# A two-part transformer kernel: order of units in two attentions, one load moved forward, the last norm per token

## The reference

```python
# first attention: 4 differential heads (qa, ka, va) and 8 grouped heads (qb, kb, vb)
oa = _rmsnorm(oa, subln) * (1.0 - lam_init)          # norm per head, over 128 features
qb = _axial_rope(_rmsnorm(qb, qk_norm[0]), ang_r, ang_c)
mix = concatenate([oa, ob]); h = h + mix @ w_out
# block attention (the third): 8 heads of 128
k = rotary(k, ...); q = rotary(q, ...) ; s = where(k_pos <= q_pos, q k, -inf); o = softmax(s) v
# the end
y = x32 * rsqrt(mean(x32 * x32, axis=-1) + NORM_EPS) * g
```

## Time and profile before

| | us |
|---|---|
| runs | 1433.71, 1434.3, 1440.1 (median 1434.3) |
| profiled execution | 1434.04, its span 1432.2 |
| PE busy | 1361.8 |
| DVE busy | 804.8 |
| ACT busy | 570.3 |
| PE's granted clock, mean | 0.994 |

### The profile page before, as it was taken

How to read it: one execution, slowest core, us unless ns; L and a number is a source line. 1 busy time by engine, 2 the same in 40 slices (tenths; PEclk the granted TensorE clock), 3 DMA queues, 4 the chain that set the end, 5 groups by cost and what they waited for, 6 DMA issues and landing times.

```text
span 1432.2 us, 25229 instructions
## 1 busy us (share of the span) xinstructions
PE 1361.8 (95%) x9936; PEld 1062.6 (74%) x9936; DVE 804.8 (56%) x1440; ACT 570.3 (40%) x1006; POOL 174.3 (12%) x168
## 2 busy tenths in 40 slices
PE   7999899999999999999999999997999999998897
PEld 6776899999767999998989996443437678454343
DVE  6968877676776756667764866211117566311112
ACT  4566544444575544446334633111106354111111
POOL 2000264332100532314000010000000001000000
PEclk9999999999999999999999999999999999999999
DMA  9141274444314444453543679999997249999995
GB/s 391 63 177 60 109 282 177 177 174 177 119 60 158 177 177 184 184 206 132 190 164 118 234 301 366 399 426 426 413 417 327 107 174 412 371 419 426 423 412 220
DMA packets 42024, 355.42 MB, mean 248 GB/s; under 512 B 4918, under 2 KB 6326, under 8 KB 21440
## 3 DMA queue, kind: packets, MB, share of 16 engines
q1 hardware_dynamic: 40560, 349.34, 61.1%
q0 software_dynamic: 928, 4.30, 0.8%
q10 hardware_dynamic: 432, 0.32, 0.1%
HBM read 352.86 MB, written 1.09 MB: 247 GB/s over the span
## 4 chain that ended last, share of the span: by engine, by line
PE 75%; DMA 12%; DVE 7%; ACT 3%; issue 1%; POOL 1%; SPq 1%; DVEq 0%; ACTq 0%; POOLq 0%
PE psum L1945 14%; PE psum L1377 13%; PE psum L1379 13%; PE psum L1378 13%; DMA ring<-w_expert_dram 7%; PE psum L1924 3%; DMA constants_sb<-constants_dram 2%; PE psum L1442 2%; DMA arena<-w_expert_dram 1%; DVE weight_low L2676 1%; PE psum L1410 1%; PE psum L1779 1%; PE psum L1778 1%; PE psum L1780 1%; DMA ring<-w_dense_dram 1%
## 5 line engine op out<-in xcount | busy, mean ns | idle before, releaser
L1377 PE MATMUL psum<-x_high,weight_low 128*128 128x256 f32 (+1 forms) x1096 | 317.9, 290 | 8.3 <-DVE x_low L2816 2.4
L2676 DVE TENSOR_TENSOR weight_low<-ring,weight_high 128x1024 fp32r<-128x1024 f32 x196 | 251.1, 1292 | 114.2 <-ACT weight_high L2200 113.6
L1378 PE MATMUL psum<-x_low,weight_high 128*128 128x256 f32 (+1 forms) x1096 | 311.3, 284 | 0.0
L1379 PE MATMUL psum<-x_high,weight_high 128*128 128x256 f32 (+1 forms) x1096 | 310.6, 283 | 0.0
L2200 ACT ACTIVATE weight_high<-ring 128x1024 fp32r<-128x1024 f32 x196 | 204.8, 1055 | 147.2 <-PE psum L1379 109.7
L1377 PEld LDWEIGHTS psum<-x_high,weight_low 128*128 128x128 f32 x1096 | 205.8, 188 | 20.5 <-issue 8.2
L1378 PEld LDWEIGHTS psum<-x_low,weight_high 128*128 128x128 f32 x1096 | 206.2, 188 | 0.8 <-issue 0.5
L1379 PEld LDWEIGHTS psum<-x_high,weight_high 128*128 128x128 f32 x1096 | 206.7, 189 | 0.0
L1945 PE MATMUL psum<-ring,xn 128*32 128x512 f32 (+2 forms) x800 | 141.2, 594 | 5.7 <-DMA ring<-w_expert_dram 5.6
L1377 PE MATMUL psum<-hidden_high,weight_low 128*128 128x272 f32 (+1 forms) x512 | 145.9, 285 | 0.2 <-DVE hidden_low L2878 0.2
L1379 PE MATMUL psum<-hidden_high,weight_high 128*128 128x272 f32 (+1 forms) x512 | 146.0, 285 | 0.0
(11 more groups left out here) (411 smaller groups left out, 2485.3 us busy)
## 6 DMA issues: line engine op xcount, KB each, us to landing
ring<-w_dense_dram SPq DMA_DIRECT2D x68, 2048.0 KB, 7.7
ring<-w_expert_dram SPq DMA_DIRECT2D x30, 2048.0 KB, 23.0
ring<-w_expert_dram SPq DMA_DIRECT2D x34, 1024.0 KB, 12.3
ring<-w_expert_dram SPq DMA_DIRECT2D x64, 512.0 KB, 12.1
ahead_a<-w_expert_dram SPq DMA_DIRECT2D x6, 2048.0 KB, 9.8
arena<-w_expert_dram SPq DMA_DIRECT2D x6, 2048.0 KB, 14.3
arena<-w_expert_dram SPq DMA_DIRECT2D x22, 512.0 KB, 19.7
constants_sb<-w_expert_dram SPq DMA_DIRECT2D x5, 2048.0 KB, 16.8
```

Of the source, the lines that this page charges most:

```text
L1377: pe.matmul(o, wl[:, c % 4, cols], high, start=start, stop=False)
L1378: pe.matmul(o, wh[:, c % 4, cols], low, start=False, stop=False)
L1379: return pe.matmul(o, wh[:, c % 4, cols], high, start=False, stop=stop)
L2676: v.tensor_tensor(split_view(wl, (name, j), c), quarter_view((name, j), q), split_view(wh, (name, j), c).bitcast(F32), ALU.subtract).then_ ...
```

## The change

Four groups of edits. In the first attention the last value block moves from unit 14 to 15, its transpose from 16 to 22, the last rotation from 5 to 7, half product 6 from 24 to 23. In the block attention the transposes at s = 5 and 7 use bank 7, and SP issues the constants before `kv` 2 instead of after `kv` 3. The root's activation table is loaded in each expert stage's last step instead of at the end. The last norm sums the squares into one column for each half of the tokens, with tokens on the partitions, takes root and reciprocal of 128x2 numbers, puts them on a diagonal (`ident` times factor), and spreads them over the partitions by a product with ones into bank 2, which DVE reads in its four products. Odd chunks are stored from ACT's queue, even ones from SP's.

```diff
-    BLOCK0 = {4 * j + x: (name, j) for j in range(4) for x, name in enumerate(("qa", "ka", "va"))}
-    TURN_V0 = {4: 0, 8: 1, 12: 2, 16: 3}
-    ROT0 = {1: 1, 3: 2, 5: 3}
-    HALF0 = {n + (16 if n < 6 else 18): n for n in range(8)}
+    BLOCK0 = {4 * j + x + (4 * j + x == 14): (name, j) for j in range(4) for x, name in enumerate(("qa", "ka", "va"))}
+    TURN_V0 = {4: 0, 8: 1, 12: 2, 22: 3}
+    ROT0 = {1: 1, 3: 2, 7: 3}
+    HALF0 = {n + (16 if n < 6 else 17 if n == 6 else 18): n for n in range(8)}
...
-                put(("mturn", s - 2), 2)
+                put(("mturn", s - 2), 7 if s in (5, 7) else 2)
...
-            load(key, extra)
-            if key == ("kv", 3):
+            if key == ("kv", 2):
                 again = slice(CONST["rotm"][0], CONST["causal"][1])
                 sp.wait_ge(moe[0]["pe"], 6 * 5)
                 sp.dma_start(cst[:, again], A["constants"][:, again]).then_inc(again_loaded, 16)
+            load(key, extra)
...
-        for c in range(KC):
+        for c in range(0, KC, 2):
             sp.wait_ge(out_ready, c // 2 + 1)
             sp.dma_start(out[c * P:(c + 1) * P, :], hT[:, c, META:T0]).then_inc(out_saved, 16)
...
-        o = take(("norm", 10))
+        take(("norm", 10))
         for c in range(KC):
             pe.wait_ge(sq_ready, sq_base[10] + c // 2 + 1)
-            mm = pe.matmul(o[:, 0:REAL], const("ones"), xn[:, c, META:T0], start=(c == 0), stop=(c == KC - 1))
+            for tt in range(2):
+                mm = pe.matmul(psum[:, tt, 0:1], xn[:, c, META + tt * P:META + (tt + 1) * P], const("ones")[:, 0:1],
+                               start=(c == 0), stop=(c == KC - 1))
         mm.then_inc(psum_full, 1)
+        pe.wait_ge(factor_ready, 1)
+        for tt in range(2):
+            mm = pe.matmul(psum[:, 2, tt * P:(tt + 1) * P], const("ones"), hs[:, tt * P:(tt + 1) * P], start=True, stop=True)
+        mm.then_inc(factor_full, 1)
...
             hidden(extra + (STEPS - 1))
+            act.activation(warm, eps[:, 0:1], ACT.Sqrt)
...
-        act.activation(warm, eps[:, 0:1], ACT.Sqrt)
-        drain(("norm", 10), rms[:, 0, 0:REAL], lambda o: o[:, 0:REAL], ACT.Sqrt, bias=eps[:, 0:1], scale=1.0 / D)
+        full(("norm", 10))
+        act.activation(rtok, psum[:, 0:2, 0:1].rearrange("p a b -> p (a b)"), ACT.Sqrt, bias=eps[:, 0:1],
+                       scale=1.0 / D).then_inc(act_drained, 1)
+        for c in range(1, KC, 2):
+            act.wait_ge(out_ready, c // 2 + 1)
+            act.dma_start(out[c * P:(c + 1) * P, :], hT[:, c, META:T0]).then_inc(out_saved, 16)
...
-        link(v.reciprocal(rms[:, 1, 0:REAL], rms[:, 0, 0:REAL]))
+        link(v.reciprocal(rtok, rtok))
+        v.tensor_tensor(hs[:, 0:REAL].rearrange("p (t s) -> p t s", t=2), const("ident").unsqueeze(1).to_broadcast([P, 2, P]),
+                        rtok.unsqueeze(2).to_broadcast([P, 2, P]), ALU.mult).then_inc(factor_ready, 1)
+        v.wait_ge(factor_full, 1)
         for b in range(4):
             two = hT[:, 2 * b:2 * b + 2, META:T0]
-            v.tensor_tensor(two, two, rms[:, 1, 0:REAL].unsqueeze(1).to_broadcast([P, 2, REAL]),
+            v.tensor_tensor(two, two, psum[:, 2, 0:REAL].unsqueeze(1).to_broadcast([P, 2, REAL]),
                             ALU.mult).then_inc(out_ready, 1)
```

More of the change, by code:

```diff
@@ L937, in program @@
     out_ready, out_saved = sem("out_ready"), sem("out_saved")
+    factor_ready, factor_full = sem("factor_ready"), sem("factor_full")
     def from_use(name, per):
@@ L2155, in _ @@
         experts(1)
-        o = take(("norm", 10))
+        assert uses["norm", 10]["banks"] == (0,)
+        take(("norm", 10))
         for c in range(KC):
             pe.wait_ge(sq_ready, sq_base[10] + c // 2 + 1)
-            mm = pe.matmul(o[:, 0:REAL], const("ones"), xn[:, c, META:T0], start=(c == 0), stop=(c == KC - 1))
+            for tt in range(2):
+                mm = pe.matmul(psum[:, tt, 0:1], xn[:, c, META + tt * P:META + (tt + 1) * P], const("ones")[:, 0:1],
+                               start=(c == 0), stop=(c == KC - 1))
         mm.then_inc(psum_full, 1)
+        pe.wait_ge(factor_ready, 1)
+        for tt in range(2):
+            mm = pe.matmul(psum[:, 2, tt * P:(tt + 1) * P], const("ones"), hs[:, tt * P:(tt + 1) * P], start=True, stop=True)
+        mm.then_inc(factor_full, 1)
     @block.scalar
```

## The result

The changed kernel took 1428.2 us (median of 5 runs, 1426.7 to 1430.5), beside 1439.3 (5 runs) for the kernel before in the same comparison; the ratio is 0.9944, interval 0.9927 to 0.9960. It is not the quotient of these two medians (0.9923): of the five runs of the kernel before two lay at 1434 and three at 1439.3 to 1440.1, so their median says little. A second set gave 1427.5 (6 runs) and 0.9941 [0.9929, 0.9953]. All 67 runs of the kernel before, in all comparisons, have a median of 1436.3. So the change makes the kernel faster by about 0.6%, some 8 us; whether by more or less than half a per cent the intervals (0.40 to 0.73%, 0.47 to 0.71%) leave open. The two profiled executions differ by less: 1434.04 and 1428.37 us, spans 1432.2 and 1426.5, which is 5.7 us.

A forecast was written before the change was run, and what follows sets the result against it. TensorE, busy for 95% of the span, was taken to bound the kernel. Gains of 3.66 + 2.54 + 0.10 + 1.40 = 7.7 us from 1434.04 gave 1426.3, stated as 1426.5 us; 8-in-10 range 1424.2 to 1430.2.

The forecast's parts named there:

- the tail: After the last expert product: new last norm -0.4 us and two store queues -1.0 us, together -1.4 us.
- faster: Whole kernel: time under the half-per-cent border at 1427.1 us; chance 0.44.
- within: Whole kernel: change of no more than half a per cent, 7.2 us, either way; chance 0.53.
- Rival A: First attention gives its part back, only 1.0 us of 3.66 stays: 1429.1 us; chance 0.20.
- Rival B: Block attention: early constants help nothing, PE next waits for the second tile's weight halves: 1428.9 us; chance 0.07.
- C: Tail: stores bound by the engines, factor's way through PE costs what it saves, gain 0: 1427.8 us; chance 0.09.
- First attention: Moved rotation, value block, transpose and half product 6: output product starts 3.66 us earlier (0.67 + 1.83 + 0.57 + 0.59).
- Constants: Block attention: constants land near 1084 us, so PE's wait before the first turn of the keys goes, -2.54 us.
- The bank: Third attention: two transposes in another bank; a 0.77 us wait goes, PE waits later instead; -0.1 us.
- The sums: Last norm: 32 one-column records take 3.69 us where 16 of 256 columns took 3.62; +0.07 us.
- The product: Last norm: product with ones spreading the factors, four records of 128 columns, taking 0.66 us.
- Rival E: PE's pauses: lower-clock stretches of 3.4 us cost each, three outweigh the gains: 1436.5 us; chance 0.03.

The follow-up runs named there:

- e2_again: The kernel before with only the constants issued before the third weight tile of the block attention: 1432.7 us (11 runs), ratio 0.9976.
- e1_first: The kernel before with only the first attention's four edits: 1432.0 us (7 runs), ratio 0.9974.
- e6_one_queue: The changed kernel with all eight stores issued by SyncE, as before the change: 1427.2 us, executed once.
- b1: The kernel before, unchanged, profiled a second time: 1434.85 us.
- e3b: Second profile of the kernel before with only the new last norm, the earlier table load and the stores on two queues: 1433.1 us.
- e10: The changed kernel with four products filling PE's pause before the retention's output product and 128 columns of ones in the last sums: 1428.2 us (6 runs), ratio 0.9941.
- e8_no_rot: The changed kernel with only the rotation put back in unit 5: 1431.7 us, executed once.

## Why the prediction was right, and where it was wrong

The time (1426.5 forecast, 1428.2 measured) was in the range, and the sum of 7.7 us came near the 8.1 to 8.6 of the medians. What failed is the step from the sum to the chances, and one term, the tail. Point by point:

**The border between "faster" and "no change": wrong, and it decided the chances.** I gave 0.53 to "within" and 0.44 to "faster", since I took half a per cent (7.2 us) for "about what a measurement of this kernel can tell from no change". The runs tell far less: e2_again is faster by 3.4 us (0.24%) with an interval from 2.0 to 4.9, and the changed kernel by 0.56%, clear of no change in both sets. With a border of 2 to 3 us (the intervals reach 1.4 to 2.5 us to either side) the rivals A, B and C, at 5 to 6 us of gain, would have been "faster" as well, and so would the third of my own forecast that I counted as "within". Of these rivals A and B (0.27 together) did not come true either.

**The base: wrong, and it moved the level.** I had written that the profiled execution is 0.3 us under the median of the runs, so both bases give the same forecast. Three runs of 1433.7, 1434.3 and 1440.1 could not say that. Of 67 runs 12 are at or under 1434.04; the median is 1436.3, 2.2 us above. From there the same 7.7 us give 1428.6, beside 1428.2 measured. The base does not explain the chances: 0.5% of it is 7.2 us as well, and 1428.6 lies 0.5 us from the border (1429.1), as 1426.6 (1434.3 less 7.7) did from 1427.1. The first profile had 17 us at the lower clock; the runs of before had 26 in the mean (from their mean clock of 0.991).

**First attention, 3.66 us: right.** 3.79 measured. The rotation 0.70 (0.67), value block and its transpose's move 2.01 (1.83), half product 6 alone 1.08 (0.57 + 0.59 for it and the transpose together; the text has 0.55 where the sum has 0.57). Query block 2 started at 78.14 (78.05) behind a wait of 1.02 us (1.14) that names the rope operation; the first output product at 148.28 (148.3). At the first half product PE had no visible wait where I had kept 0.2 us. Rival A, for which I had 0.20, is refuted by e1_first.

**Constants, 2.54 us: right in mechanism, the size in part luck.** 2.82 by the two traces: the wait of 2.54, a turn shorter by 0.10, the rest beside it. But the wait that goes was 1.65 to 2.77 us in seven profiles, which makes this term an estimated 1.9 to 3.1 us. The constants landed at 1082.2, as forecast "near 1084"; the 5.25 us a tile of the working should be 5.2 by its own numbers. Rival B is refuted.

**The bank, 0.1 us: right,** the wait moved to the value product: 0.0.

**The tail, 1.4 us: the mis-sized term.** About 0.5 in the first profile, 0.4 to 0.9 in all eight with one-column sums and two queues. Three pieces failed. The sums were to take 3.69 us; they took 3.63 as long as the clock held and up to 4.34 (e6_one_queue) when it fell in them. The product was put at 0.66; it was 1.22, always at 1.2 GHz, and 0.71 with wide sums. With wide sums the first store came 0.52 us earlier relative to the sums than before, where I had 0.4: the chain was right but for the clock. And two queues gave 0.7 us, not 1.0, since the DMA engines were then busy all the time. The working of this term was also loose: -0.34 with 0.2 more is not "-0.4 at most", and the floor of 0.8 and 3.1 us leaves 1.0 only with some 0.8 us from the last packet to the end of the span, which the text does not name (in both traces it is there). The records of the router held for the spacing (3.63 us for 32 is 0.11 apart). By the Trainium skill (TensorE: Matmul & The Clock Gate, Back-to-back issue gap), whose 81 ns are stated for 128 columns, I had set an estimated 2.7 us beside this; the traces disagree, with 3.63 us for one column and 3.73 for 128.

**Rival E, the clock: its mechanism is there, its place was not.** I had argued that no pause named grows. None needed to: falls came behind pauses that the change leaves as they are (1.87 us at the retention, 2.7 to 3.5 us near 1340), in 8 of 15 and 13 of 17 profiles (the four without the second are the first profile, b1, e3b and e10). One at PE-bound work costs 1.5 us for 3.4 us at the lower level, as the earlier trace rows had suggested at 3.4 for 6.9. The pauses that the change removes had such falls behind them as well (e8_no_rot, e2_again).

**The sum.** 3.79 + 2.82 + 0.0 + 0.4 to 0.9 = 7.0 to 7.5 us of the 7.7 forecast, and 6.1 to 7.7 with the spread of the constants' wait. Between the two profiles a fall took 1.5 of it; between the medians, 8.1 to 8.6 us, about 1 us is left over, which stays open; that the forecast is so near the medians is to this extent luck. Fewer falls in the first attention could be part of it, but two in eight profiles against none in nine is too few to show it, and the mean clocks (0.990 in 11 runs of the changed kernel, 0.991 in 62 of the kernel before; the longer fall in the tail taken off) leave room for an estimated 0.4 us at most.

## What to carry to other kernels

Walking from wait to wait and asking what is late next gave each term ahead of the tail to 0.3 us between two profiles of this kernel. A single profile gives neither the base nor the size of a wait for a transfer: the one here was 1.65 to 2.77 us. And before a chance is put on "no change", ask how small a change the runs can tell: with 5 to 11 runs the intervals reached 1.4 to 2.5 us to either side here, not 7. A chain of tiny matmuls can cost more than its records show, because what follows runs at the lower clock: look at the granted clock behind it, and try wider records where the weight loads set the pace anyway (3.73 for 3.63 us here, and 0.71 for 1.22 behind them). A pause of PE of one to two microseconds in front of PE-bound work has a second price of 1.5 us that comes only in some executions. The two profiles in which it was filled with idle products did not have it, which may be chance, and the times could not be told from those without the fill.

## What was not expected of the hardware

32 records of 128 columns took 3.73 us and 32 of one column 3.63: with 128 times the columns only 0.1 us more, so the weight loads set the pace. Behind the one-column records the granted clock fell in all nine profiles before the next product, behind the wide ones in none of three, although PE counts as busy in both. Ahead of the tail all falls were 3.4 or 6.8 us long, and two profiles of the changed kernel have all of them at the same microsecond, while e6_one_queue, alike up to the stores, has none behind the retention's pause and one at 998 that they lack. What picks the execution was not found.
